# Routing and gather ahead of the first expert, split and reordered, in a four-layer kernel

## The reference

```python
# B=1, S=256 tokens, D=1024, 16 experts of width 1024, EC_CAPACITY=2
def expert_choice_ffn(xn, w_router, w_gate, w_up, w_down):
    cap = EC_CAPACITY * S // N_EXPERTS                    # 32 tokens per expert
    aff = jax.nn.softmax((xn @ w_router).astype(jnp.float32), axis=-1)
    g, idx = lax.top_k(aff.swapaxes(1, 2), cap)           # each expert its 32 best tokens
    xs = xn[bidx, idx]
    hid = silu(einsum('becd,edf->becf', xs, w_gate)) * einsum('becd,edf->becf', xs, w_up)
    y = einsum('becf,efd->becd', hid, w_down) * g[..., None]
    return zeros_like(xn).at[bidx, idx].add(y)
# xn = rms_norm(h, ffn_norm); everything is float32
```

## Time and profile before

| | us |
|---|---|
| median of three runs (lowest, highest) | 2198.19 (2194.28, 2198.45) |
| profiled execution | 2194.73 |
| its span | 2193.3 |
| TensorE busy in the span | 1880.5 (86%) |
| VectorE busy | 913.0 (42%) |
| ScalarE busy | 634.0 (29%) |
| main DMA queue, share of 16 engines | 70.7% |
| HBM read | 614.44 MB, 281 GB/s over the span |

### The profile page before, as it was taken

One profiled execution on the slowest core, in us unless ns is written; L12 is line 12 of the kernel. 1 busy time (PEld: TensorE's weight loads), 2 busy tenths in 40 slices (PEclk: granted clock), 3 DMA queues, 4 the chain that ended last, 5 costly groups with the idle time before them and its releaser, 6 DMA issues.

```text
span 2193.3 us, 31044 instructions
## 1 busy us (share of the span) xinstructions
PE 1880.5 (86%) x12852; PEld 1255.4 (57%) x12852; DVE 913.0 (42%) x1536; ACT 634.0 (29%) x1098; POOL 43.2 (2%) x46
## 2 busy tenths in 40 slices
PE   6999999999999999999898866666798996756666
PEld 3887888987888889988655311112275552212112
DVE  3675576645576576646753100000068530000001
ACT  3244235545245136534451100000055310000001
POOL 0001000000002000000000000000000000000000
PEclk9999999999999999999999978888899999788778
DMA  9565348556533354453658999999983789999997
GB/s 337 213 231 193 117 154 307 193 192 224 198 129 142 117 177 169 187 196 66 236 204 351 427 427 425 429 426 427 420 267 128 306 358 426 427 427 425 429 425 330
DMA packets 120006, 617.50 MB, mean 282 GB/s; under 512 B 18448, under 2 KB 21434, under 8 KB 86586
## 3 DMA queue, kind: packets, MB, share of 16 engines
q1 hardware_dynamic: 119290, 613.85, 70.7%
q10 hardware_dynamic: 576, 1.66, 0.2%
HBM read 614.44 MB, written 1.05 MB: 281 GB/s over the span
## 4 chain that ended last, share of the span: by engine, by line
PE 59%; DMA 28%; DVE 9%; ACT 2%; issue 1%; SPq 0%; POOL 0%; DVEq 0%; ACTq 0%
PE pb L706 57%; DMA ring<-in_w_up_dram 17%; DMA ar<-in_w_up_dram 4%; DMA hT<-in_w_up_dram 4%; PE pb L709 2%; DVE ar L1639 2%; DVE ar L1647 2%; DMA ring<-in_w_down_dram 1%; DVE small L1655 1%; DMA ring<-in_ada_w_dram 1%; DVE ar L1643 1%; DVE ar L1651 1%; ACT ar L2441 1%; DVE small L1643 0%; DVE ws L1639 0%
## 5 line engine op out<-in xcount | busy, mean ns | idle before, releaser
L706 PE MATMUL pb<-ring,ar 128*32 128x512 f32 (+1 forms) x2128 | 360.9, 726 | 185.0 <-DMA ring<-in_w_up_dram 140.7
L706 PE MATMUL pb<-ar 64*64 64x64 f32 (+10 forms) x3760 | 438.1, 372 | 74.5 <-DMA hT<-in_w_up_dram 35.9
L2445 ACT COPY ar<-pb 128x512 f32<-128x512 f32 (+2 forms) x195 | 112.7, 578 | 920.5 <-PE pb L706 868.5
L1651 DVE COPY ar<-pb 128x512 f32<-128x512 f32 (+5 forms) x98 | 58.7, 599 | 722.2 <-PE pb L706 707.7
L706 PEld LDWEIGHTS pb<-ar 64*64 64x64 f32 (+5 forms) x3760 | 212.0, 144 | 242.2 <-issue 224.0
L706 PEld LDWEIGHTS pb<-ring,ar 128*32 128x32 f32 (+1 forms) x2128 | 96.6, 132 | 396.2 <-issue 385.3
L706 PE MATMUL pb<-hT,ring 128*128 128x256 f32 x1024 | 235.4, 386 | 0.4 <-ACT ar L2441 0.4
L706 PEld LDWEIGHTS pb<-hT,ring 128*128 128x128 f32 x1024 | 193.0, 192 | 33.6 <-issue 7.8
L1639 DVE TENSOR_TENSOR ws<-ring,ws 128x1024 fp32r<-128x1024 f32 x128 | 156.9, 1226 | 124.0 <-ACT ws L2445 122.2
L706 PE MATMUL pb<-hs,ws 128*128 128x256 f32 x1536 | 187.0, 284 | 2.5 <-ACT aux L2445 1.5
L706 PEld LDWEIGHTS pb<-hs,ws 128*128 128x128 f32 x1536 | 185.6, 193 | 4.3 <-ACT aux L2445 1.7
(11 more groups left out here) (168 smaller groups left out, 1647.9 us busy)
## 6 DMA issues: line engine op xcount, KB each, us to landing
ring<-in_w_down_dram SPq DMA_DIRECT2D x46, 2048.0 KB, 27.8
ring<-in_w_gate_dram SPq DMA_DIRECT2D x42, 2048.0 KB, 28.4
ring<-in_w_up_dram SPq DMA_DIRECT2D x40, 2048.0 KB, 23.4
ring<-in_w_mlp_dram SPq DMA_DIRECT2D x32, 2048.0 KB, 7.7
ring<-in_w_in_dram SPq DMA_DIRECT2D x27, 2048.0 KB, 9.2
ring<-in_ada_w_dram SPq DMA_DIRECT2D x24, 2048.0 KB, 8.5
ar<-in_w_gate_dram SPq DMA_DIRECT2D x12, 2048.0 KB, 20.4
ar<-in_w_up_dram SPq DMA_DIRECT2D x12, 2048.0 KB, 23.2
```

What stands on the lines that cost most here:

```text
L706: return e.matmul(o, l, r, start=start, stop=stop)
L1651: return e.tensor_copy(o, i)
L2445: return e.copy(o, i)
```

## The change

- `Pm0` and the front gather take experts 0 and 1 (64 columns) instead of 0 to 3. A new `second()` gathers experts 2 and 3, 64 columns for each `c` into one bank `xs_b`, behind `gate_up(0)`. `Pm` is built for fourteen experts before that.
- `rest()` and `scatter(0)` move, on TensorE, from between `gate_up(2)` and `down(1)` to behind `hidden(2)`. VectorE's and ScalarE's parts of `rest()` move behind their parts of `hidden(2)` as well.
- Routing: the two subtractions of the maxima become one product of `mx`, -1 and `rstd`, used as a bias by the exponential, which reads PSUM and adds up its outputs; the reduction goes. The comparison behind the last `match_replace` moves behind `sel`, in the place of a copy. `iota` counts from 1, so one need not be taken from the slots. `Pm` and the scaling of `xs0` on VectorE are written with fewer operations on larger tiles.
- `SPARE`: seven matmuls instead of six ahead of `sel`, three instead of one ahead of the gather.
- The order in which places are handed on: the place of `("gu", l, 2, 0)` now comes behind those of `down` of expert 0. So the fifth and sixth block take the places of `down` of expert 0, and the seventh that of `("gu", l, 2, 0)`.

```diff
-    two["iota"] = np.broadcast_to(np.arange(32), (128, 32))
+    two["iota"] = np.broadcast_to(np.arange(1, 33), (128, 32))
...
-    ("aff",): (2, 2), ("chosen",): (6, 6), ("Pm0",): (1, 1),
+    ("aff",): (2, 2), ("chosen",): (7, 7), ("Pm0",): (3, 3),
...
-                for first in sorted((f for f in first_at if f[1] == name[1]), key=lambda f: (f[0] != "gu", f)):
+                for first in sorted((f for f in first_at if f[1] == name[1]), key=lambda f: (f[2] > 1, f[0] != "gu", f)):
...
-                    m = tr(pb[:, 16 * t:16 * t + 16], rt1_[:, 128 * t:128 * t + 128])
+                    m = tr(pb[:, 16 * t:16 * t + 16], rt0[:, 128 * t:128 * t + 128])
...
-                        m = gather(c, 0, 4, pb, 128 * (c % 4))
+                        m = gather(c, 0, 2, pb, 64 * (c % 4))
...
+                def second():
+                    e.wait_ge(*V("Pm", l))
+                    k, pb = bank("xs_b", l)
+                    for c in range(8):
+                        m = gather(c, 2, 2, pb, 64 * c)
+                    m.then_inc(*P.up("xs_b", l))
+                    psum.until(k, V, "xs_b", l)
...
                     if s < 16:
                         gate_up(s)
-                    if s == 2:
-                        rest()
-                        acc += [bank("moe", l, n) for n in range(4)]
-                    if s >= 2:
+                    if s == 0:
+                        second()
+                    if s > 2:
                         scatter(s - 2)
                     if 1 <= s <= 16:
                         down(s - 1)
                     if s < 16:
                         hidden(s)
+                    if s == 2:
+                        rest()
+                        acc += [bank("moe", l, n) for n in range(4)]
+                        scatter(0)
...
-                for t in range(2):
-                    m = ts(aff[:, t, :], ps("router", l, t)[:, 0:16], mx[:, t:t + 1], None, ALU.subtract)
-                    m.then_inc(*(V.up("logits", l) if t else step()))
+                stt(mx, mx, -1.0, rstd[:, :], ALU.mult, ALU.mult).then_inc(*V.up("logits", l))
                 e.wait_ge(*A("aff_e", l, 1))
-                reduce(smv, aff, ALU.add).then_inc(*step())
...
-                ts(rt1_, rt0, 0.0, None, ALU.is_lt).then_inc(*V.up("chosen", l))
                 e.wait_ge(*P("sel", l))
-                copy(sel, v4(ps("sel", l)[:, 0:32], 2)).then_inc(*V.up("sel", l))
+                ts(sel, v4(ps("sel", l)[:, 0:32], 2), 0.0, None, ALU.is_lt).then_inc(*V.up("sel", l))
...
-                ts(pm, pm, -1.0, None, ALU.add).then_inc(*step())
...
+                def selecting(e0, n, name):
+                    P4 = Pm[:, :, e0:e0 + n]
+                    tt(P4, bc(K2("iota").unsqueeze(1).unsqueeze(1), [128, 2, n, 32]),
+                       bc(pm3[:, :, e0:e0 + n].unsqueeze(3), [128, 2, n, 32]), ALU.is_equal).then_inc(*step())
+                    tt(P4, P4, bc(rstd[:, :].unsqueeze(2).unsqueeze(2), [128, 2, n, 32]), ALU.mult).then_inc(*V.up(name, l))
+
+                def gathered(to, c0, nc, src):
+                    shape = [128, nc, to.shape[2]]
+                    return tt(to[:, c0:c0 + nc, :], v4(src, nc), bc(fncol[l][:, c0:c0 + nc].unsqueeze(2), shape), ALU.mult)
+                selecting(0, 2, "Pm0")
                 e.wait_ge(*P("xs0", l, 0))
+                gathered(xs0[:, :, 0:64], 0, 4, ps("xs0", l, 0)[:, 0:256]).then_inc(*V.up("xs0", l, 0))
+                selecting(2, 14, "Pm")
+                e.wait_ge(*P("xs_b", l))
+                gathered(xs0[:, :, 64:128], 0, 8, ps("xs_b", l)[:, :]).then_inc(*V.up("xs_b", l))
...
-                    act(aff[:, t, :], aff[:, t, :], ACT.Exp, scale=rstd[:, t:t + 1]).then_inc(*A.up("aff_e", l, t))
+                    act(aff[:, t, :], ps("router", l, t)[:, 0:16], ACT.Exp, bias=S("r_mx", 2)[:, t:t + 1], scale=rstd[:, t:t + 1],
+                        accum=S("r_sm", 2)[:, t:t + 1]).then_inc(*A.up("aff_e", l, t))
...
-                    m = gathered(c, 0, 4, ps("xs0", l, 1)[:, 128 * (c - 4):128 * (c - 4) + 128])
+                    m = gathered(xs0[:, c, 0:64], c, ps("xs0", l, 1)[:, 64 * (c - 4):64 * (c - 4) + 64])
```

More of the change, by code:

```diff
@@ L89 @@
     "group": "stat g_sum xg",
-    "route": "router logits aff_e aff affT chosen sel slot Pm0 Pm xn xs0 xs1 PA PW",
+    "route": "router logits aff_e aff affT chosen sel slot Pm0 Pm xn xs0 xs_b xs1 PA PW",
     "norm": "root normed",
@@ L1492, in z_route @@
                     for t in range(2):
-                        psum.until(psum.at["router", l, t], V, "logits", l)
+                        psum.until(psum.at["router", l, t], A, "aff_e", l, t)
             def experts(l):
@@ L1549, in gate_up @@
                         e.wait_ge(*V("xs0", l, 0))
+                    if x_ == 2:
+                        e.wait_ge(*V("xs_b", l))
                     if x_ == 4:
@@ L2347, in experts @@
                 tt(pm3, v4(ps("slot", l)[:, 0:32], 2), sel, ALU.mult).then_inc(*V.up("slot", l))
-                ts(pm, pm, -1.0, None, ALU.add).then_inc(*step())
-                for e0, n, name in ((0, 4, "Pm0"), (4, 12, "Pm")):
-                    for t in range(2):
-                        m = tt(Pm[:, t, e0:e0 + n], bc(K2("iota").unsqueeze(1), [128, n, 32]),
-                               bc(pm3[:, t, e0:e0 + n].unsqueeze(2), [128, n, 32]), ALU.is_equal).then_inc(*step())
-                    for t in range(2):
-                        m = ts(Pm[:, t, e0:e0 + n], Pm[:, t, e0:e0 + n], rstd[:, t:t + 1], None, ALU.mult)
-                        m.then_inc(*(V.up(name, l) if t else step()))
-                def gathered(c, e0, n, src):
-                    return ts((xs1 if e0 else xs0)[:, c, :], src, fncol[l][:, c:c + 1], None, ALU.mult)
+                def selecting(e0, n, name):
[7 more added lines that the diff above has]
+                selecting(0, 2, "Pm0")
                 e.wait_ge(*P("xs0", l, 0))
-                for c in range(4):
-                    m = gathered(c, 0, 4, ps("xs0", l, 0)[:, 128 * c:128 * c + 128])
-                    m.then_inc(*(V.up("xs0", l, 0) if c == 3 else step()))
+                gathered(xs0[:, :, 0:64], 0, 4, ps("xs0", l, 0)[:, 0:256]).then_inc(*V.up("xs0", l, 0))
+                selecting(2, 14, "Pm")
+                e.wait_ge(*P("xs_b", l))
+                gathered(xs0[:, :, 64:128], 0, 8, ps("xs_b", l)[:, :]).then_inc(*V.up("xs_b", l))
                 def rest():
@@ L2374, in rest @@
                         e.wait_ge(*P("xs1", l, c))
-                        gathered(c, 4, 12, ps("xs1", l, c)[:, 0:384]).then_inc(*V.up("xs1", l, c))
+                        ts(xs1[:, c, :], ps("xs1", l, c)[:, 0:384], fncol[l][:, c:c + 1], None, ALU.mult).then_inc(*V.up("xs1", l, c))
                     for gp in range(0, 8, 2):
@@ L2900, in experts, with gathered @@
                 for t in range(2):
-                    act(aff[:, t, :], aff[:, t, :], ACT.Exp, scale=rstd[:, t:t + 1]).then_inc(*A.up("aff_e", l, t))
-                def gathered(c, e0, n, src):
-                    return act((xs1 if e0 else xs0)[:, c, :], src, ACT.Copy, scale=fncol[l][:, c:c + 1])
+                    act(aff[:, t, :], ps("router", l, t)[:, 0:16], ACT.Exp, bias=S("r_mx", 2)[:, t:t + 1], scale=rstd[:, t:t + 1],
+                        accum=S("r_sm", 2)[:, t:t + 1]).then_inc(*A.up("aff_e", l, t))
+                def gathered(to, c, src):
+                    return act(to, src, ACT.Copy, scale=fncol[l][:, c:c + 1])
                 e.wait_ge(*P("xs0", l, 1))
                 for c in range(4, 8):
-                    m = gathered(c, 0, 4, ps("xs0", l, 1)[:, 128 * (c - 4):128 * (c - 4) + 128])
+                    m = gathered(xs0[:, c, 0:64], c, ps("xs0", l, 1)[:, 64 * (c - 4):64 * (c - 4) + 64])
                     m.then_inc(*(A.up("xs0", l, 1) if c == 7 else step()))
@@ L2912, in rest @@
                         e.wait_ge(*P("xs1", l, c))
-                        gathered(c, 4, 12, ps("xs1", l, c)[:, 0:384]).then_inc(*A.up("xs1", l, c))
+                        gathered(xs1[:, c, :], c, ps("xs1", l, c)[:, 0:384]).then_inc(*A.up("xs1", l, c))
                     for gp in range(1, 8, 2):
```

4 lines of the change are left out of this document (2 added, 2 removed).

## The result

| | before | after |
|---|---|---|
| median of 8 runs each (lowest, highest), us | 2194.44 (2192.75, 2198.45) | 2204.67 (2201.73, 2206.54) |
| profiled execution, us | 2194.73 | 2206.12 |
| its span, us | 2193.3 | 2204.8 |
| mean granted clock of TensorE | 0.935 | 0.929 |

A forecast was written before the change was run, and what follows sets the result against it. The DMA queue of weight blocks bounds the expert stages. Per layer, routing -1.36 and late slots +2.4 give +1.0, both layers +2.1 us on a median of 2198.19: 2200.3 us, own range 2197 to 2203, stated range 2190 to 2207.

The forecast's parts named there:

- The bound and the restart: Expert stages last as long as the DMA queue's blocks; its restart after routing, if earlier, shortens each layer equally.
- T: Start of `gate_up(0)`, 1168.87 us in layer 0 before the change; the prediction counts block issues from it.
- The routing chain: Routing operations ahead of the front gather: 1.36 us earlier per layer, bounds 0.8 and 1.8, filler cost of 0.2 included.
- The gather's pace: Front gather: 0.24 us for each of 32 records, set by weight loads, so halving moving columns saves nothing.
- The columns rival: Moving columns set the gather's pace: both gathers take 3.9 us, 10.5 us gained, 2187.7 us; chance 0.13.
- The gaps: Late slots behind the second gather starve the queue: 1.0 us at fourth block, 0.3 at fifth, 2.4 per layer in all.
- What the sort key buys: Fifth block takes the slot of `down` of expert 0; with the old slot order it would come six microseconds later.
- The clock: Rival: narrow gathers lower TensorE's clock for `gate_up(0)` and `gate_up(1)`, 1.6 us at each, two layers; 2202 to 2207, chance 0.24.
- The likeliest case: The forecast itself: shorter routing, unchanged gather pace, late slots, 2200.3 us, own range 2197 to 2203; chance 0.40.
- the twelfth slot is in time: Rival: no gap at the twelfth block, `("gu", l, 4, 1)`, so only the shorter routing counts: 2195.5 us; chance 0.13.
- `PA`: Rival of another late wait: VectorE's eight products exceed their 3 us of slack, 2203 us and above; chance 0.10.
- The sum: Per layer -1.36 for routing and +2.4 for late slots make +1.0; both layers +2.1 us.

The follow-up runs named there:

- The kernel with 128 columns: Changed kernel with both gathers streaming their 64 columns twice, into a second copy nobody reads; 2197.66 us beside 2194.06 for before, ratio 1.0014.
- the old order of places: Changed kernel with both gathers streaming their 64 columns twice, and the sort key of before; 2205.48 us beside 2195.70 for before, ratio 1.0043.
- neighbouring columns in all gathers: Changed kernel with 128 neighbouring columns as stationary operand of every gather, values then wrong; 2185.25 us beside 2194.06 for before, ratio 0.9957.
- for the first four experts: One front gather on neighbouring columns, short routing, only experts 0 to 3's gate and up blocks reordered; 2181.18 us beside 2194.56 for before, ratio 0.9939.
- 128 columns in `second()` alone: Changed kernel with only the second gather streaming its 64 columns twice, the front one narrow; 2200.49 us beside 2195.70 for before, ratio 1.0024.

## Why the prediction was right and where it was wrong

**The bound and the restart: right.** In every kernel that leaves the layout of the weight blocks alone the queue is full at 427 GB/s from behind the twelfth block to the end of the stage, and what differs among them lies ahead of it. Wherever the clock stayed up the restart is issued 3.7 us behind T.

**The routing chain: right in layer 0, wrong in layer 1.** 1.38 us against the predicted 1.36, with a filler cost of 0.35 instead of 0.2 (`Pm0` ends at 1161.69, the fillers let the gather start at 1162.04). The kernel with 128 columns has 1.37 in both layers. In layer 1 of the changed kernel only 0.06 was left. Its timeline shows what the text had excluded ("the seventh filler ahead of `sel` ends well before the comparison does"):

```profile
1748.30 5.93 PE L706 MATMUL pb<-c 128*128 128x256 f32 x14
...
1752.40 0.40 DVE L2349 MATCH_REPLACE8 ar<-ar 16x256 f32<-16x256 f32 x1
...
1754.16 0.29 PE L709 MATMUL pb<-c,ar 16*128 16x16 f32 x2
```

```profile
1748.30:1754.16 5.86, 5.86 (x15) 4.39 (x14) 3.97 (x13) 0.00 (x0) 0.00 (x0) 0.53 0.99 421
```

Seven fillers at a clock of 0.53 take 5.9 us (3.19 in layer 0) and let `sel` start 1.36 us behind the end of the last match-replace, where layer 0 has 0.05. I had timed them at the upper level. It is no accident of this execution: nine kernels here have seven and three fillers, one trace of two layers each, and in four of these eighteen layers (the changed kernel and the old order of places in layer 1, neighbouring columns in all gathers and for the first four experts in layer 0) the seven take 5.8 to 5.9 us and `sel` is some 1.3 us late. In a fifth (128 columns in `second()` alone, layer 1) the three take 2.91 us instead of 1.54 and hold the gather 1.7 us beyond `Pm0`. In the six layers with six and one neither happens.

**The gather's pace: right.** 7.52 and 7.73 us for 32 records with 64 columns, 0.24 us each, the same at either level of the clock; it is the weight load, and the load is slow because of the stride (328 against 192 ns with nothing else changed). The columns rival is out. The Trainium skill's LDWEIGHTS rule in TensorE: Matmul & The Clock Gate (columns over 1.2, so 107 ns for 128), by which the gather would have taken an estimated 3.4 us, has no term for the stride. The strided gather does not agree with it; the one with neighbouring columns comes near, 3.7 us for 32 records or 0.12 us each. The loads' own records are longer than this pace, since they overlap: 32 of 192 ns fit into 3.7 us of busy time, and 32 of 328 into 7.5. So 328 against 107 ns, which the prediction compared, is not like with like.

**The gaps: the places right, their sizes shared out wrongly.** With the clock up the fourth, fifth and twelfth blocks were issued within 0.4, 0.4 and 0.7 us of the predicted moments. The queue lost 1.8 us about the fourth and fifth and 0.3 to 0.45 about the twelfth, where the text had 1.3 and then 1.1 more; over T+5.4 to T+100 it lost 2.7 us in either layer against 0.9 and 1.1 before, a rise of 1.8 and 1.6 us against the predicted 2.4. The share under 0.9 that was to show at both places is 0.94 and 0.99 in windows of 12 us. What the sort key buys was right too: the fifth block six microseconds earlier, 6.4 us of the time measured.

**The clock: this step failed.** The likeliest case had the clock of `gate_up(0)` and `gate_up(1)` at 1.00, argued from "the 128-column gather kept 1.00, and more filler stands ahead of it". The first half compares the wrong thing: pace and busy time of the two gathers are equal, but not the columns that they stream, and the kernel with 128 columns differs from the changed one otherwise only in the two banks of its second gather and the two operations that scale it. The second half doesn't help, since one gather with the same filler keeps 1.00 and the split one with either filler doesn't. The rival's mechanism came in all four places. Its price of 1.6 us each was slightly low: the first half of `gate_up(0)` took 5.72 and 5.29 instead of 3.70 us (2.0 and 1.6), that of `gate_up(1)` with its `hidden(0)` 6.5 and 6.3 instead of 4.3 (2.2 and 2.0). "Each paid in full" holds: the twelfth block is 4.2 and 3.5 us later against T than with 128 columns. What about the fewer columns brings the clock down no run shows.

**The other rivals.** That the twelfth slot is in time did not come: each kernel with a second gather of 7.7 us has its gap there or at the fourth; with the 3.8 us of neighbouring columns there is none. `PA` was not late either. TensorE's eight products of 128x512 begin behind the same wait for ScalarE, with the same 0.87 us of idle time as before:

```profile
1225.88 3.67 PE L706 MATMUL pb<-ar 128*128 128x512 f32 x8 [0.87 <-ACT ar L2455]
```

**The sum.** Predicted +2.1 us without the clock; the kernel with 128 columns has +3.1 (1.1 to 5.0). That the two are close is in part luck: chain and queue account for only 1.8 + 1.6 - 2 x 1.37 = +0.7 of the 3.1 in its trace, since the gap was smaller than predicted, and what makes up the rest is open. With the clock +9.7, of which 8.5 are accounted for by chain and queue in one execution. The first operation behind the maxima of layer 0 starts between 1149.79 and 1153.92 us in the twelve kept traces, 4 us apart, and the rest is not resolved against that.

## What to carry to other kernels

A gather that is paced by its weight loads, as this one is, gains nothing from fewer moving columns and can lose the clock for the work behind it; take the stride out of the stationary operand first (7.5 to 3.7 us here), and look at the granted clock behind the stretch, not only in its middle. Filler ahead of a step is to be timed at the lower clock as well: seven matmuls that took 3.2 us at the upper level took 5.9 and delayed the step. When one engine's work is put ahead of slots that feed a saturated DMA queue, find for each slot the moment of its issue against the moment at which the queue runs dry: moving the work moved the gap here, and the order of the slots or less work made it smaller. A layout that helps one operand but cuts the DMA into shorter pieces is to be used only for the blocks that need it (13.4 us faster for four experts, 11 slower for sixteen).

## What the runs showed of the hardware that I had not expected

- TensorE's clock falls to the lower level while its records are busy without a gap: with 64 moving columns each 0.24 us it fell in both gathers, with 128 at the same pace it stayed, and with 64 at 0.12 us (neighbouring columns) it stayed as well. The ends of the records are modelled.
- Loading a 128x128 float32 operand with a stride of four elements takes 328 ns against 192 contiguous, and such loads follow each other every 0.24 us against 0.12.
- On a full queue blocks of which two thirds came in pieces of 4 KB moved at 415 GB/s, and with all in pieces of 16 KB at 427, both at a DMA share of 1.01 to 1.02. With 4 KB for the gate and up blocks of four experts of sixteen the later blocks moved at 429; this is not explained.
